# Seams of a recurrent layer re-ordered, and the products of its scan alternated over four quadrants of the array

## The reference

```
for both layers: shift, scale, gate = split(silu(cond) @ ada_w + ada_b)     # "adaln"
u = modulate(x, norm_g, shift, scale) @ w_in      # gate | rwkv | hyena | hyena gate
# rwkv branch: two directions over 256 context + 512 tokens, 8 heads of 64
sa = einsum('bhij,bhj->bhi', s, kk_t)
s  = s * w_t - sa * b_t + v_t * k_t
y  = einsum('bhij,bhj->bhi', s, r_t)
# y of both directions is group-normed, gets a bonus term, is gated
# hyena branch: a short convolution, filters from a small net, two long convolutions by FFT
x = x + gate * (concat(rwkv, hyena) @ w_out)
```

## Time and profile before

| | |
|---|---|
| median of three runs | 3194.7 us |
| the profiled execution | 3200.95 us |
| its span in the trace | 3199.1 us |
| TensorE busy | 2862.5 us, 89% |
| TensorE weight loads | 2210.9 us, 69% |
| VectorE busy | 1529.5 us, 48% |
| ScalarE busy | 1069.8 us, 33% |
| GpSimd busy | 131.3 us, 4% |
| mean granted TensorE clock | 0.942 |
| moved by DMA | 224.39 MB, mean 70 GB/s |

### The profile page before, as it was taken

One profiled execution on the slowest core, in us unless ns is written; L12 is line 12 of the kernel. 1 busy time (PEld: TensorE's weight loads), 2 busy tenths in 40 slices (PEclk: granted clock), 3 DMA queues, 4 the chain that ended last, 5 costly groups with the idle time before them and its releaser, 6 DMA issues. The chain is left out here.

```text
span 3199.1 us, 53678 instructions
## 1 busy us (share of the span) xinstructions
PE 2862.5 (89%) x23146; PEld 2210.9 (69%) x23146; DVE 1529.5 (48%) x2511; ACT 1069.8 (33%) x1933; POOL 131.3 (4%) x122
## 2 busy tenths in 40 slices
PE   7899988988989998778999998898887988899997
PEld 3588766766767886356887876566656866788876
DVE  5623247344446665674555233455445436445422
ACT  6411367332224443213222232554224132422222
POOL 0000000000012453000000000000000000000000
PEclk9899999989989999898999999999888999899999
DMA  8412200134100002202332223312211122223321
GB/s 312 129 53 60 44 1 1 53 111 127 55 1 4 4 4 59 82 1 92 92 99 86 91 76 107 94 58 63 60 59 38 47 79 74 66 86 93 93 87 65
DMA packets 221629, 224.39 MB, mean 70 GB/s; under 512 B 27345, under 2 KB 192721, under 8 KB 221330
## 3 DMA queue, kind: packets, MB, share of 16 engines
q1 hardware_dynamic: 221090, 219.78, 22.6%
q10 hardware_dynamic: 304, 1.18, 0.1%
HBM read 207.61 MB, written 12.80 MB: 69 GB/s over the span
## 5 line engine op out<-in xcount | busy, mean ns | idle before, releaser
L212 DVE TENSOR_TENSOR second_w_low<-second_w_raw,second_w_high 128x1024 fp32r<-128x1024 f32 (+1 forms) x236 | 282.2, 1197 | 493.0 <-ACT second_w_high L208 492.3
L208 ACT CAST second_w_high<-second_w_raw 128x1024 fp32r<-128x1024 f32 (+1 forms) x236 | 241.4, 1025 | 695.7 <-PE ffn_in_acc L233 248.5
L231 PE MATMUL ffn_in_acc<-ffn_h_high,second_w_high 128*128 128x512 f32 x704 | 281.1, 399 | 6.6 <-DVE ffn_h_low L674 6.0
L232 PE MATMUL ffn_in_acc<-ffn_h_low,second_w_high 128*128 128x512 f32 x704 | 278.5, 396 | 0.0
L233 PE MATMUL ffn_in_acc<-ffn_h_high,second_w_low 128*128 128x512 f32 x704 | 278.4, 395 | 0.0
L212 DVE TENSOR_TENSOR first_w_low<-first_w_raw,first_w_high 128x1024 fp32r<-128x1024 f32 x91 | 110.7, 1223 | 256.1 <-ACT first_w_high L208 255.8
L208 ACT CAST first_w_high<-first_w_raw 128x1024 fp32r<-128x1024 f32 x91 | 94.5, 1046 | 209.1 <-PE attn_in_acc L233 80.2
L231 PEld LDWEIGHTS ffn_in_acc<-ffn_h_high,second_w_high 128*128 128x128 f32 x704 | 134.0, 190 | 38.2 <-issue 8.8
L231 PE MATMUL attn_in_acc<-attn_h_high,first_w_high 128*128 128x256 f32 (+1 forms) x416 | 144.0, 346 | 14.4 <-DVE attn_h_low L406 14.4
L233 PEld LDWEIGHTS ffn_in_acc<-ffn_h_high,second_w_low 128*128 128x128 f32 x704 | 134.1, 190 | 30.0
L232 PEld LDWEIGHTS ffn_in_acc<-ffn_h_low,second_w_high 128*128 128x128 f32 x704 | 134.1, 191 | 29.8 <-issue 0.7
(11 more groups left out here) (830 smaller groups left out, 6360.3 us busy)
## 6 DMA issues: line engine op xcount, KB each, us to landing
second_w_raw<-in_ffn_w_gate SPq DMA_DIRECT2D x44, 512.0 KB, 3.8
second_w_raw<-in_ffn_w_up SPq DMA_DIRECT2D x44, 512.0 KB, 3.8
second_w_raw<-in_ffn_w_down SPq DMA_DIRECT2D x40, 512.0 KB, 3.5
first_w_raw<-in_rec_w_in SPq DMA_DIRECT2D x33, 512.0 KB, 3.9
second_w_raw<-in_w_in SPq DMA_DIRECT2D x24, 512.0 KB, 3.9
second_w_raw<-in_w_branch_gate SPq DMA_DIRECT2D x24, 512.0 KB, 4.0
first_w_raw<-in_attn_w_in SPq DMA_DIRECT2D x22, 512.0 KB, 3.9
first_w_raw<-in_attn_ada_w SPq DMA_DIRECT2D x12, 512.0 KB, 8.1
```

The lines of the kernel that those rows point to most:

```text
L208: act.copy(self.view(self.high[b % self.splits], b), self.view(self.raw[self.ring[b]], b)).then_inc(self.high_done, 1)
L212: dve.tensor_tensor(self.view(self.low[b % self.splits], b), self.view(self.raw[self.ring[b]], b), self.view(self.high[b % self.splits], b ...
L231: pe.matmul(out, sh, mh, start=(first and j == 0), stop=False)
L232: pe.matmul(out, sh, ml, start=False, stop=False)
```

## The change

The change has three parts.

1. **adaln.** The high and low parts of the two condition vectors are put side by side as four stationary columns. A block takes four products in place of six; the transposes and four more additions sum the halves. `InputRoots` squares as before, but sums with the matrix of ones as stationary operand (two products of 512 and 256 columns a step), so that the sums stand on all partitions; ScalarE takes the root of 128x768, and VectorE inverts it in three parts of 128x256. The column, the diagonal and the spreading product are gone.
2. **The seams.** The context's split moves into `hy_in` (`SplitAside`). The zeroing stages become two or three small memsets ahead of the next stage (`zero_ends`). The stores of `hy_in` are no longer waited for at its end: VectorE waits at step 4 of `rwkv_in`, SyncE before the small loads, which are issued at the end of `rwkv_in`'s weight loads. The load of `spread` is issued at the end of `hy_in`. After the scan the filter tables go first (with the clearing by GpSimd ahead of `late`), then the gate, the transform tables, the weight blocks, and the first half of `x`. The second half of `x` is loaded before `rec_out`; each half is waited for when `rec_out` first adds to it (`x_back`).
3. **The scan.** Logs and turns become products of 64x64 over four quadrants, turns now with `eye` as the moving operand. Three steps that used two quadrants (`z`, `value`, `solved`) use four. The products `rate` (next group) and `gate` (the one after) alternate. Two turns stand ahead of `z`. The products that read the state (`scan_read`) come straight behind `scan_sa`. `value` now waits for ScalarE's `z`.

```diff
 class InputRoots:
     def pe(self, pe, step):
-        if 8 <= step < 8 + KD:
-            self.root.add(pe, step - 8, self.squares[(step - 8) % 4])
-        if step == 19:
-            self.root.spread_over(pe, self.spread)
+        k = step - 8
+        if 0 <= k < KD:
+            pe.wait_ge(self.squared, k + 1)
+            for t0, tn in spans(TT, BANK):
+                ins = pe.matmul(self.sums[:, t0:t0 + tn], self.c["ones"], self.squares[k % 4][:, t0:t0 + tn],
+                                start=(k == 0), stop=(k == KD - 1))
+            ins.then_inc(self.summed, 1)
     def dve(self, dve, step):
-        if step == 18:
-            self.root.make_diag(dve)
+        if step in (18, 20, 22):
+            at = slice(128 * (step - 18), 128 * (step - 16))
+            dve.wait_ge(self.rooted, 1)
+            dve.reciprocal(self.root_out[:, at], self.root_out[:, at])
...
+                    if stacked:
+                        half, out = slice(t0, t0 + rows // 2), ps[n % slots][:, 0:sum(widths)]
+                        for j, k in enumerate(ks):
+                            pe.matmul(out[0:rows], x(k)[:, at], high[:, j, :], start=(k == 0), stop=False, skip_group_check=True)
+                            ins = pe.matmul(out[0:rows // 2], x(k)[:, half], low[:, j, :], start=False, stop=(k == kc - 1),
+                                            skip_group_check=True)
...
+class SplitAside:
+    def act(self, act, n, wait_stored):
+        if n < KD:
+            act.wait_ge(self.scaled, n + 1)
+            self.feed.high(act, n).then_inc(self.made_high, 1)
+    def dve(self, dve, n):
+        if n < KD:
+            self.feed.scale(dve, n).then_inc(self.scaled, 1)
+        if 1 <= n <= KD:
+            dve.wait_ge(self.made_high, n)
+            self.feed.low(dve, n - 1)
...
+    def pe_rate_beside_gate(self, pe, n, rate, gate):
+        for i in range(4):
+            at = slice(i * P, (i + 1) * P)
+            rates = pe.matmul(rate[:, at], self.up_a[self.rows(n), at], self.lora_a[self.rows(n), self.at(n)], start=True, stop=True)
+            gates = pe.matmul(gate[:, at], self.lora_w[self.rows(n + 1), self.at(n + 1)], self.up_w[self.rows(n + 1), at],
+                              start=True, stop=True)
...
-            ins = pe.matmul(room[:, i * P:(i + 1) * P], self.log_w[n % 2][:, i * P:(i + 1) * P], of, start=True, stop=True)
+            for f in range(2):
+                for k in range(2):
+                    r, to, at = slice(CH * k, CH * k + CH), slice(CH * f, CH * f + CH), i * P + CH * f
+                    ins = pe.matmul(room[to, k * BANK + CH * i:k * BANK + CH * i + CH], self.log_w[n % 2][r, at:at + CH], of[r, k, :],
+                                    start=True, stop=True)
...
 RWKV_PE = Marks("four", "step4", "eight", "step8", "step16", "ux", "mh", "wx", "gram_k", ... "turn0", "turn1", "z", "turn2",
-            def turn(n, s, ps):
+            def turn(n, s, ps, first, crossed=0):
                 for i in range(PAIRS):
-                    ins = pe.transpose(ps[:, i * P:(i + 1) * P], f[:, s, i, :], c["ident"])
+                    for h in range(2):
+                        for k in range(2):
+                            at = h * BANK + first + i * CH
+                            ins = pe.matmul(ps[rows(k ^ (h & crossed)), at:at + CH], f[rows(h), s, i, rows(k)], eye[rows(h), :],
+                                            start=True, stop=True)
...
+                turn(n, 0, out_ps, 0, 1)
+                turn(n, 2, out_ps, 256)
                 pe.wait_ge(act_done, RWKV_ACT(n, "wx0"))
                 pe.wait_ge(dve_done, RWKV_DVE(n, "wx1"))
-                tiles(late, 0, wx[:, 1], wx[:, 0], 0, 0).then_inc(pe_done, 1)
...
+                tiles(late, 0, wx[:, 1], wx[:, 0], 0, 1).then_inc(pe_done, 1)
+                turn(n, 3, sa_ps, 0)
             def value(n):
                 pe.wait_ge(dve_done, RWKV_DVE(n, "gram_k1"))
+                pe.wait_ge(act_done, RWKV_ACT(n, "z"))
...
-                tiles(late, 0, z, av, 0, 0).then_inc(pe_done, 1)
+                tiles(late, 0, z, av, 1, 0).then_inc(pe_done, 1)
...
-    zero(nc, "rwkv_pad", [padded])
+        zero_ends(nc, ends_zeroed, [padded[:, :, 0:1], padded[:, :, S + 1:S + 3], padded[:, :, PADDED - 1:PADDED]])
+        if n == 4:
+            hy_saved.wait(dve)
...
-            queue.wait_ge(saved, 64)
+            load_spread(queue)
...
-            returned.start(gate[:], d["s_rec_gate"].rearrange("(i p) t -> p i t", p=P))
             second = second()
-            second.start()
             with ExitStack() as filters:
                 tables = filter_loads(nc, d, filters, hidden)
+                returned.start(gate[:], d["s_rec_gate"].rearrange("(i p) t -> p i t", p=P))
+                tables["load_transform"]()
+                second.start()
+                back[0].start(x[:, 0:4], saved_x[:, 0:4])
...
-        back = Ahead(nc, keep, "rec_back")
-        back.start(x[:], d["s_x"].rearrange("(k p) t -> p k t", p=P))
-        back.wait(nc.vector)
+        back[1].start(scanned, saved_x[:, 4:8])
...
+        def x_back(dve, n, stored):
+            if n in (0, 4):
+                back[n // 4].wait(dve)
```

More of the change, by code:

```diff
@@ L2079, with rwkv_gate_loads @@
 CUM = CH + 1
-def rwkv_gate_loads(nc, d, stack, vec_at, up_w, up_a):
-    loads = Ahead(nc, stack, "rwkv_up")
+def rwkv_gate_loads(d, loads, vec_at, up_w, up_a, queue):
     for up, weights, rows in ((up_w, "rwkv_w_up", "w0_rows"), (up_a, "rwkv_a_up", "a0_rows")):
@@ L2422, in both, with by_head, by_pair @@
             return ps.rearrange("p (h n) -> p h n", h=2)[:, :, first:first + 256]
+        def by_head(part):
+            return part.rearrange("p i (h t) -> p h i t", h=2)
+        def by_pair(ps, first):
+            return both(ps, first).rearrange("p h (i t) -> p h i t", t=CH)
         def by_bank(part):
@@ L2608, in scan_new @@
                 if tile < 4:
+                    if step == 0 and n < last:
+                        pe.wait_ge(dve_done, RWKV_DVE(n + 1, "diag_x"))
                     for i in range(PAIRS):
@@ L2613, in scan_new @@
                                       start=(step == 0 and i == 0), stop=False, skip_group_check=True)
+            def scan_new(n, step):
+                dr, tile = groups[n]
+                r = rows(order(dr)[step])
                 pe.wait_ge(scan_dve, SCAN(n, f"sa{step}"))
@@ L2646, in _ @@
             of.pe_gate(pe, 1, bank(out_ps, 0))
-            of.pe_logs(pe, 0, bank(late, 0))
+            of.pe_logs(pe, 0, late)
             pe.wait_ge(of.opened, 2)
@@ L2903, in _ @@
             of.act_gate(act, 1, bank(out_ps, 0))
-            of.act_exps(act, 0, bank(late, 0))
+            of.act_exps(act, 0, late)
             of.act_bonus(act, 0)
@@ L2992, in shift @@
         return ins
-    linear(nc, "rwkv_in", w, *h, TT, evict, engines="a", after=(shift, 13), aside=aside)
+    linear(nc, "rwkv_in", w, *h, TT, evict, engines="a", after=(shift, 13), aside=aside, save=loads)
 def products(nc, name, jobs, engines=2, slots=6):
@@ L3177, in _ @@
                 tap(n)
-            pe.wait_ge(landed, 16)
+            tables["spreads"].wait(pe)
             pe.wait_ge(inverted, 1)
@@ L3353, in save @@
                     queue.wait_ge(stored["a"], 16)
-                queue.dma_start(out[:, 4 * i:4 * i + 4], part).then_inc(saved, 16)
-            queue.wait_ge(saved, 64)
-        linear(nc, "hy_in", w, *h, S, evict, engines="a", after=(convolve, 12), save=save)
+                saved.start(out[:, 4 * i:4 * i + 4], part, queue)
+            load_spread(queue)
+        linear(nc, "hy_in", w, *h, S, evict, engines="a", after=(convolve, 12), save=save, aside=aside)
 def hyena_branch(c, v, nc, tables, spectrum, root, inputs, spare, out):
@@ L4453, in rec_layer @@
         y = sb("y", [P, KD, S])
+        back = [Ahead(nc, keep, f"rec_back{i}") for i in range(2)]
+        saved_x, scanned = d["s_x"].rearrange("(k p) t -> p k t", p=P), x[:, 4:8, :]
         flat_x, flat_y, flat_ctx = (t.rearrange("p k t -> p (k t)") for t in (x, y, ctx))
@@ L4484, in rec_layer, with load_spread @@
-                    gate_loads = rwkv_gate_loads(nc, d, shifted, v.where, up_w, up_a)
                     spread = flat_gate[0:8, 2 * TT:2 * TT + 512]
-                    spreads = Ahead(nc, shifted, "rwkv_spread")
-                    for engine in (nc.sync, nc.vector, nc.scalar):
+                    spreads, hy_saved = Ahead(nc, shifted, "rwkv_spread"), Ahead(nc, shifted, "hyena_saved")
+                    gate_loads = Ahead(nc, shifted, "rwkv_up")
+                    def load_spread(queue):
+                        spilled.wait(queue)
+                        spreads.start(spread, d["c_spread2"][0:8, 0:4 * P], queue)
@@ L4488, in rec_layer, with load_ups @@
                         spilled.wait(engine)
-                    spreads.start(spread, d["c_spread2"][0:8, 0:4 * P])
+                    def load_ups(queue, followed, stored):
```

(4 more changed lines are left out.)

181 lines of the change are left out of this document (101 added, 80 removed).

## The result

The changed kernel takes 3176.3 us (median of five), the kernel before 3198.2 in the same comparison: a ratio of 0.9926, with an interval of 0.9901 to 0.9951. Forecast were 3133 and a range from 3112 to 3158, so the gain is some 22 us where 61 were counted. The profiled execution took 3182.52 us against 3200.95, 18.4 less.

| part | forecast, us | measured, us | from, to |
|---|---|---|---|
| adaln, by the start of `attn_in` | -6 | +0.1 | 117.58, 117.67 |
| seam `rec_gate` to `hy_in` | -7.7 | -7.8 | 8.75, 0.94 |
| seam `hy_in` to `rwkv_in` | -9.0 | -8.9 | 10.85, 2.00 |
| clock: lengths of `hy_in` and `rwkv_in` | -4 | -3.0 | 91.98 + 136.58, 89.47 + 136.05 |
| `late` | -10.5 | -11.7 | 88.03, 76.35 |

A forecast was written before the change was run, and what follows sets the result against it. TensorE, busy 89% of the span, was taken as the bound, with time in its waits at seams and excess products. Terms -6 - 7.7 - 9.0 - 4 - 10.5 - 9.0 - 15 = -61 gave 3133.5 us on the median, range 3112 to 3158.

The forecast's parts named there:

- four mechanisms: Waits removed at `hy_in` (-7.7 us), `rwkv_in` (-9.0), in `late` (-10.5) and ahead of `rec_out` (-9.0).
- the clock behind them: In `hy_in` and `rwkv_in`: shorter gaps keep TensorE at the higher clock level, -4 us (0 to -4.5).
- TensorE's own work falls by 1.4 to 2.2 us a group: Scan: shorter quadrant steps save TensorE this much, of which 1.4 us a group was counted over 11 groups.
- -15 forecast: Scan: total gain of 15 us, bounded by -25 and +5.
- the overlap of row halves within one bank: Scan: `z`, `value` and `solved` gain although their row halves share a bank; without it the scan's sum would be -4.
- The new waits: Scan: `value` waits for `z`'s eviction, 0.3 us, and the next products for two turn copies, 0.5 us.
- The turns stay level: Scan: 12 transposes in 1.46 us against three four-quadrant steps of 0.47 us each, so no change.
- the sum was made at the last product: adaln: savings less inversions and links give -6 us (-14 to +1), its last product near 95.
- the links: adaln: four more links of the additions cost under 1 us.
- C: Rival: one or two seams don't close; with two open and no scan gain, -27 us, 3168; chance 0.08.
- D: Rival: the scan falls to 1.2 GHz as TensorE waits more often; at 40% it is +40, 3235; chance 0.04.

The follow-up runs named there:

- e4: Kernel before with every edit of the scan and nothing else: scan 336.0 us, whole 3214.9 us, ratio 1.0057.
- e1: Changed kernel with its scan put back as before, adaln and seams still changed: scan 314.6 us, whole 3149.6 us, ratio 0.9855.
- e5: Kernel before with three runs of products that wait for nothing added at the scan's end: first run 36.9 us, third 36.5.
- e9: Kernel before with two turns and the logs of the scan as uncrossed quadrant products, adding records: scan 325.1 us, ratio 1.0027.
- e6: Changed kernel with logs and two turns whole, 64 by 128 products in the first turn, one-product gate, adaln's last sums moved earlier: 3172.6 us, 0.9902.
- e7: e1 with state reads ahead, `rate` beside a one-product `gate`, and adaln's last sums moved out earlier: scan 318.5 us, whole 3151.5, ratio 0.9836.
- e12: e7 without the state reads ahead, so `rate` beside `gate` is the scan's only edit: scan 315.5 us, whole 3148.7, ratio 0.9844.
- e10: Changed kernel with logs and two turns whole again, state reads and `rate`, `gate` order as before: scan 322.8 us, whole 3151.9, ratio 0.9856.
- e11: Kernel before with four runs of first-turn product shapes added at the scan's end: 1.02, 0.43, 0.42 and 0.22 us a pair.
- e8: Kernel before with only the adaln part changed: `attn_in` starts at 115.39 us, whole at ratio 0.9972.

## Why the prediction was wrong

**The seams were right**: four mechanisms, what is late next behind each, and the sizes to within 1.2 us (table above). The forecast for the clock behind them was right for `hy_in` (2.5 us shorter) and wrong for `rwkv_in`: after 2.00 us without work its fourth product is back at 0.63 us (granted clock 0.50), and the stage gives 0.5 in place of 2.

**The scan was wrong, in the term that was not there.** The step that failed is "TensorE's own work falls by 1.4 to 2.2 us a group" as the whole of TensorE's bill. That part held: net of issue waits the scan fell by 15 us in each of the two like comparisons (e4 against before, after against e1), with -15 forecast. So did the overlap of row halves within one bank, against the rule of the Trainium skill that the prediction weighed ("TensorEngine Tiling (Array Packing)", section "Gotcha 1: PSUM Pressure"): `z`, whose row halves share a bank, went from 1.18 to 0.80 us (no row tells which of its products overlap). The new waits cost what was said or less: `value` 3.0/12 = 0.25 us a group for `z`, and the grams 1.1 us in all. What was missing is that the same work in quadrants comes as 1356 more records (9480 to 10836), and records have a supply. The bill leaves out 30 us more of issue waits (e4 against before) or 46 (after against e1), and these turn the -15 into a longer scan. The earlier trace rows held the sign of it, 2.3 us of "issue" in one row and 1.6 in another, and the text left both unread. "The turns stay level" was the dearest sentence: in TensorE's time they are nearly so (1.46 us a group before, 1.75 after, idle time left out), but they carry 84 of the 114 records a group.

The size follows roughly from e5. Before, a packet's 128 records took 314.1/9480 x 128 = 4.24 us net, above the 3.72 that a packet needs there; after, 295.0/10836 x 128 = 3.48. At 3.72 us a packet the 10836 records take 315 us, however evenly the products come. That is an estimate: in the scan after, the fastest nine packets in a row are 3.55 us apart, by which it would be 301. What the scans have above 315, 21 us in e4 and 30 in the kernel after, I put down to products that come in bursts at up to 16 ns a record, with waits for VectorE between; no run separates that. e9 lies just above 3.72 (3.81 net) and has 14 us of issue waits; all kernels under 4.0 have 14 or more, and those at 4.2 have 4 to 7. e6, slow for another reason, is the exception (4.31 and 14.9). Why the same scan has 13 us more issue waits in the kernel after than in e4 stays open; that the packets' ends fall on other products is only argued.

**adaln was wrong by its end.** The products ended at 95.9, near the 95 forecast, but the sum was made at the last product. What is late next there, the landing and split of `attn_in`'s first weights (2.5 us lost), was not asked for in that part. Nor was the clock: TensorE stands longer ahead of the turn, and the turn runs at 0.50 (+1.9). Only the links were in the sum.

**The rivals.** C's time, 3168, is the nearest, but for another reason: C had two seams open, and all closed. D had a scan that gets slower, by a mechanism that did not occur: the granted clock was 0.98 to 1.00 from 940 to 1180 us, and 0.96 over the scan against 0.95 before. The range had no rival in which more instructions cost time.

## What to carry to other kernels

When an edit splits products into smaller ones, count instructions as well as array time: compare the records a us with what the instruction queue brings, and read every "<-issue" that recurs at a constant number of records as supply. Near that limit an edit pays in waits for what it gains in array time. But an edit that adds no instruction is no gain by that alone: those of e7 and e12 gave nothing. Here the seams with the old scan are as good as anything run (e1, e12 and e7, and with the crossing e10: 3149 to 3152 us, ratios 0.9836 to 0.9856, which can't be told apart). And a stage ends with its last engine: carry each gain through to the start of the next stage's products before it goes into the sum.

## What the runs showed of the hardware

- TensorE's instructions come in packets of 16 KB, 128 matmul records with their weight loads. In e5's first run there is one each 3.72 us, some 34 records a us, and in the scan after the fastest nine in a row are 3.55 us apart. With the clock at 0.50 it is 3.81 (e5, third run), most of which is array time. A run of products that takes less than some 29 ns a record outruns the 3.72.
- An issue wait of this kind ends 1.2 to 1.6 us behind the landing of a packet (all 51 in the scan after, all 9 before).
- Products of 64 by 64 by 64 alternated over four quadrants take 16 ns a record when supplied (2.09 us for 128, e5), and about as long with 8 columns (229 in 3.55 us). From one row half alone, at the 0.50 clock, they take 56 ns (5.38 us for 96, e11).
- A change between a 64 by 128 and a 64 by 64 tile costs 0.37 us for each pair of heads at the 0.50 clock (1.02 against 0.43 + 0.22, e11).
- 33-row products in the lower and upper rows run side by side whether they alternate one by one (after) or stand as one of 512 columns and four of 128 (e7): 1.16 us for both in either form, where they took 1.68 one behind the other before.
- The same 48 small products of adaln's turn take 5.25 us at a granted clock of 0.50 (after) and 3.63 where the clock falls 2.2 us into them (e8).
